# The inverse roots of all norms of a four-layer trunk: tokens across the partitions in place of tokens along the columns

## What is computed

```python
def rms_norm(x, g):
    xf = x.astype(F32)
    y = xf * lax.rsqrt(jnp.mean(xf * xf, axis=-1, keepdims=True) + EPS)
    return (y * g.astype(F32)).astype(x.dtype)
```

## Time and profile before

| | us |
|---|---|
| three timed runs | 3506.8, 3507.42, 3504.56 |
| median | 3506.8 |
| profiled execution, first to last instruction | 3502.8 |
| TensorE busy (matmul) | 3042.4 (87%) |
| TensorE busy (weight load) | 2847.5 (81%) |
| VectorE busy | 2287.8 (65%) |
| GpSimd busy | 1537.3 (44%) |
| ScalarE busy | 935.4 (27%) |

### The profile page before, as it was taken

The page is one execution under the profiler, slowest core; times in us unless marked ns, Lnnn a source line. Parts: engine busy times, 40 slices in busy tenths (PEclk is TensorE's granted clock), DMA queues, the critical chain, the costliest instruction groups (busy, mean ns, idle before and its releaser), DMA issues.

```text
span 3502.8 us, 62449 instructions
## 1 busy us (share of the span) xinstructions
PE 3042.4 (87%) x24344; PEld 2847.5 (81%) x24344; DVE 2287.8 (65%) x3035; ACT 935.4 (27%) x1276; POOL 1537.3 (44%) x670
## 2 busy tenths in 40 slices
PE   5788899999788799989454469999999999989999
PEld 5555599999788699989444469999998988789999
DVE  5566568861677758881699975888144345478850
ACT  3122233332433233332100113333221221122221
POOL 4111055565222155555445435555643332356663
PEclk9789899999899899999677779999999999999999
DMA  3001022233111122223100002222332222112232
GB/s 110 25 27 33 19 79 84 86 107 98 60 54 48 36 73 84 84 85 103 54 1 0 0 15 89 78 87 87 112 103 77 82 67 73 55 56 89 84 104 83
DMA packets 66509, 235.52 MB, mean 67 GB/s; under 512 B 8144, under 2 KB 9040, under 8 KB 65616
## 3 DMA queue, kind: packets, MB, share of 16 engines
q1 hardware_dynamic: 63648, 225.77, 21.3%
q10 hardware_dynamic: 2736, 7.94, 0.7%
HBM read 231.58 MB, written 2.10 MB: 67 GB/s over the span
## 4 chain that ended last, share of the span: by engine, by line
PE 46%; DVE 36%; issue 13%; DVEq 2%; ACT 1%; POOL 1%; DMA 0%; ACTq 0%; POOLq 0%
PE ps L224 36%; DVE scr L426 7%; DVE scr L423 6%; DVE ub L417 4%; DVE scr L420 3%; PE ps L237 2%; DVE work L1550 2%; PE ps L245 1%; PE ps L1810 1%; DVEq L420 1%; DVE work L1046 1%; PE ps L990 1%; DVE spare L1546 1%; DVE work L792 1%; DVE scr L1538 1%
## 5 line engine op out<-in xcount | busy, mean ns | idle before, releaser
L224 PE MATMUL ps<-xs,wr 128*128 128x264 f32 x13056 | 1659.5, 288 | 71.3 <-POOL xs L336 31.6
L224 PEld LDWEIGHTS ps<-xs,wr 128*128 128x128 f32 x13056 | 1623.0, 192 | 105.0 <-issue 61.5
L212 POOL TENSOR_TENSOR wr<-raw,wr 128x1024 fp32r<-128x1024 f32 x422 | 1103.5, 2617 | 1291.0 <-ACT wr L204 1288.2
L224 PE MATMUL ps<-hid,wr 128*128 128x264 f32 x6528 | 803.4, 286 | 28.2 <-POOL wr L212 13.8
L224 PEld LDWEIGHTS ps<-hid,wr 128*128 128x128 f32 x6528 | 799.0, 190 | 32.3 <-POOL wr L212 15.6
L204 ACT ACTIVATE wr<-raw 128x1024 fp32r<-128x1024 f32 x422 | 442.1, 1050 | 442.2 <-PE ps L224 438.6
L426 DVE SCALAR_TENSOR_TENSOR scr<-ub,convp,scr 128x528 f32<-128x528 f32 x176 | 469.2, 2666 | 24.0 <-DVE scr L423 0.6
L443 DVE TENSOR_TENSOR h<-ps,h 128x528 f32 x32 | 22.7, 708 | 358.1 <-PE ps L224 357.7
L487 POOL TENSOR_TENSOR hid<-scr,hid 128x528 f32 x88 | 137.3, 1561 | 222.8 <-ACT hid L459 222.8
L423 DVE SCALAR_TENSOR_TENSOR scr<-ub,convp,scr 128x528 f32<-128x528 f32 x176 | 205.2, 1166 | 26.6 <-DVE scr L420 17.4
L1363 PE MATMUL ps<-spare,work 128*128 128x256 f32 (+1 forms) x288 | 83.5, 460 | 131.5 <-ACT spare L1618 131.2
(11 more groups left out here) (265 smaller groups left out, 2643.2 us busy)
## 6 DMA issues: line engine op xcount, KB each, us to landing
raw<-in_stream SPq DMA_DIRECT2D x422, 512.0 KB, 3.6
work<-in_ret_tab ACTq DMA_DIRECT2D x4, 1056.0 KB, 5.5
h<-in_h SPq DMA_DIRECT2D x8, 264.0 KB, 5.8
out<-h SPq DMA_DIRECT2D x8, 256.0 KB, 4.6
work<-in_s_b ACTq DMA_DIRECT2D x1, 1024.0 KB, 5.1
work<-in_s_c ACTq DMA_DIRECT2D x1, 1024.0 KB, 6.8
convp<-in_convp ACTq DMA_DIRECT2D x4, 88.0 KB, 1.9
work<-in_mla_tab ACTq DMA_DIRECT2D x1, 264.0 KB, 2.6
```

The costliest lines, as they stand in the source:

```text
L212: pool.tensor_tensor(wr[:, s, 1].rearrange("p a b -> p (a b)"), raw[:, s, :], wr[:, s, 0].rearrange("p a b -> p (a b)").bitcast(F32), ALU. ...
L224: mm = pe.matmul(out[:, q], wr[:, slot, w, b0 + k], x[k][v][:, q * HALF:(q + 1) * HALF], start=start and k == 0 and p == 0, stop=stop and ...
```

## The change

`sums_pe` swaps its operands: the squares, a block of 128 tokens, are the stationary operand, and one column of ones is the moving one. The result has the tokens on the partitions, one column for each of five blocks of tokens. The last block begins at token 400, so that it overlaps the fourth. The first operand's quarters and the tile positions go. `mean_rsqrt` works on 128 x 5, or 128 x 10 for the two norms of an MLA head, and its last product is one instruction into a small tile; the memsets that cleared the old destinations go. `spread_pe` has five matmuls: the stationary operand is one column of the roots repeated 128 times by a stride of zero, the moving operand is the identity matrix, which yields each token's root on every partition in its column. The spread tile is then contiguous (528 columns), no longer two halves, and the readers' views change with it.

```diff
         def sums_pe(pe, g, col, srcs):
-            for q in range(4):
+            for b in range(COLS):
+                t0 = min(b * P, T - P)
                 for j, (src, rows) in enumerate(srcs):
-                    mm = pe.matmul(flat(g)[32 * q:32 * q + 32, col:col + QUARTER], ones[0:rows, 0:32],
-                                   src[0:rows, q * QUARTER:(q + 1) * QUARTER],
-                                   start=j == 0, stop=j == len(srcs) - 1, tile_position=(0, 32 * q))
+                    mm = pe.matmul(flat(g)[:, col + b:col + b + 1], src[0:rows, t0:t0 + P], ones[0:rows, 0:1],
+                                   start=j == 0, stop=j == len(srcs) - 1)
             return mm
 
-        def spread_pe(pe, g, quarters):
-            for q in range(2):
-                mm = pe.matmul(tile(g)[:, q], pick[:], quarters[:, q * HALF:(q + 1) * HALF], start=True, stop=True)
+        def spread_pe(pe, g, r):
+            for b in range(COLS):
+                t0, first_row = b * P, max(0, b * P - (T - P))
+                w = min(P, T - t0)
+                mm = pe.matmul(flat(g)[:, t0:t0 + w], r[:, b:b + 1].broadcast_to([P, P]), ident[:, first_row:first_row + w],
+                               start=True, stop=True)
             return mm
 
-        def mean_rsqrt(dve, g, cols, width, quarters, scratch, o, pre, r=0, free=None):
-            n = len(cols) * QUARTER
+        def mean_rsqrt(dve, g, col, n, width, dst, scratch, o, pre, r=0, free=None):
...
-            for k, c in enumerate(cols):
-                ins = dve.tensor_scalar(x[:, k * QUARTER:(k + 1) * QUARTER], flat(g)[:, c:c + QUARTER], 1.0 / width, EPS,
-                                        ALU.mult, ALU.add)
-                if k < len(cols) - 1:
-                    one(f"mean{k}", ins, False)
+            ins = dve.tensor_scalar(x, flat(g)[:, col:col + n], 1.0 / width, EPS, ALU.mult, ALU.add)
...
-            for k, dst in enumerate(quarters):
-                for q in range(4):
-                    rows, c = slice(32 * q, 32 * q + 32), slice(k * QUARTER, (k + 1) * QUARTER)
-                    one(("q", k, q), dve.scalar_tensor_tensor(dst[rows, q * QUARTER:(q + 1) * QUARTER], t[rows, c], 1.5,
-                                                              y[rows, c], ALU.add, ALU.mult), False)
+            one("r", dve.scalar_tensor_tensor(dst, t, 1.5, y, ALU.add, ALU.mult), False)
...
         def norm_dve(dve, n, g):
-            dve.memset(rstd[:], 0.0).then_inc(norm_dve_done.sem, norm_dve_done.one("clear"))
             dve.wait_ge(norm_pe_done.sem, norm_pe_done.done("sums", n))
-            dve.wait_ge(norm_dve_done.sem, norm_dve_done.done("clear", n))
-            mean_rsqrt(dve, g, [SUMS], D, [rstd], ub[:, 1, 2:], norm_dve_done, "n", n)
+            mean_rsqrt(dve, g, SUMS, COLS, D, rcol[:, 0:COLS], ub[:, 1, 2:], norm_dve_done, "n", n)
             dve.memset(sqsum[:], 0.0).then_inc(sum_cleared, 1)
             dve.wait_ge(norm_pe_done.sem, norm_pe_done.done("spread", n))
-            dve.tensor_copy(halves(rstd[:]), tile(g)).then_inc(tile_free, 1)
+            dve.tensor_copy(rstd[:], flat(g)[:, 0:T]).then_inc(tile_free, 1)
```

More of the change, by code:

```diff
@@ L39 @@
 QB = SEQ // P
-QUARTER = T // 4
 SUMS = 848
 NEWTON = ["bits", "y0", "a0", "b0", "y1", "a1", "b1", "y2", "a2", "b2"]
-RSQRT = ["mean"] + NEWTON + [("q", 0, q) for q in range(4)]
-LAST = ("q", 0, 3)
+COLS = 5
+RSQRT = ["mean"] + NEWTON + ["r"]
+LAST = "r"
 HEADS = 8
@@ L146, in trunk @@
         ident = sb("ident", [P, P])
+        rcol = sb("rcol", [P, 8])
         gains = sb("gains", [P, 2 * DEPTH, DT])
@@ L167, in trunk @@
         norm_pe_done = Order(sem("norm_pe"), ["sums", "spread"])
-        norm_dve_done = Order(sem("norm_dve"), ["clear"] + [("n", s) for s in RSQRT])
+        norm_dve_done = Order(sem("norm_dve"), [("n", s) for s in RSQRT])
         sum_cleared = sem("sum_cleared")
@@ L291, in norm_spread_pe @@
             pe.wait_ge(norm_dve_done.sem, norm_dve_done.done(("n", LAST), n))
-            spread_pe(pe, g, rstd).then_inc(norm_pe_done.sem, norm_pe_done.one("spread"))
+            spread_pe(pe, g, rcol).then_inc(norm_pe_done.sem, norm_pe_done.one("spread"))
         def first_tiles_pe(pe, n, u0, g):
@@ L514, in mla @@
             fac = work[:, 16]
-            scratch = work[:, 18:20].rearrange("p a b -> p (a b)")
-            quarters = [work2[:, (10 + k) * T:(11 + k) * T] for k in range(2)]
+            scratch = misc[:, 112:142]
+            rhead = misc[:, 100:100 + 2 * COLS]
             prob = [work[:, 26 + k] for k in range(2)]
@@ L522, in mla @@
             lsq = [work[:, 10 + k] for k in range(5)]
-            lquarters = [work[:, 15], work[:, 17]]
+            lrows = [misc[:, 144 + 8 * k:144 + 8 * k + COLS] for k in range(2)]
             groups = ((0, 3, QL), (3, 5, KVL))
-            SUM_Q, SUM_K = 512 + P, 512 + P + QUARTER
+            SUM_Q, SUM_K = 512 + P, 512 + P + COLS
             G_Q, G_QR, G_K, G_KR = 5, 6, 7, 8
@@ L542, in mla @@
             consts_in = sem("mla_consts")
-            l_dve = Order(sem("mla_l_dve"), ["clear0", "clear1"] + [(k, s) for k in range(2) for s in RSQRT] +
-                          [("norm", t) for t in (0, 1, 3)] + ["gain", "up", "down", "turned", "clearq", "cleark"])
+            l_dve = Order(sem("mla_l_dve"), [(k, s) for k in range(2) for s in RSQRT] +
+                          [("norm", t) for t in (0, 1, 3)] + ["gain", "up", "down", "turned"])
             l_act = Order(sem("mla_l_act"), [("square", t) for t in range(6)] + [("hi", t) for t in range(5)])
@@ L548, in mla @@
             p_dve = Order(sem("mla_p_dve"), ["up", "down", "turned", "vt", "vtm"] +
-                          [("f", s) for s in ["mean0"] + NEWTON + [("q", k, q) for k in range(2) for q in range(4)]] +
+                          [("f", s) for s in RSQRT[1:]] +
                           ["qr", "kn", "kr"])
@@ L602, in pe_ @@
                     pe.wait_ge(l_dve.sem, l_dve.done((k, LAST)))
-                    spread_pe(pe, g0 + 7 + k, lquarters[k]).then_inc(l_pe.sem, l_pe.one(f"spread{k}"))
+                    spread_pe(pe, g0 + 7 + k, lrows[k]).then_inc(l_pe.sem, l_pe.one(f"spread{k}"))
                 pe.wait_ge(l_pool.sem, l_pool.done(("lo", 4)))
@@ L631, in proj @@
                         k = int(s == "spreadk")
-                        pe.wait_ge(p_dve.sem, p_dve.done(("f", ("q", k, 3)), h0) + i * 2 * len(p_dve.names))
-                        spread_pe(pe, g, quarters[k]).then_inc(p_pe.sem, p_pe.one(s))
+                        pe.wait_ge(p_dve.sem, p_dve.done(("f", LAST), h0) + i * 2 * len(p_dve.names))
+                        spread_pe(pe, g, rhead[:, k * COLS:(k + 1) * COLS]).then_inc(p_pe.sem, p_pe.one(s))
                 def attend(s, j, h0, i, g):
@@ L689, in dve_ @@
                 dve.wait_ge(consts_in, 32)
-                for k in range(2):
-                    dve.memset(lquarters[k], 0.0).then_inc(l_dve.sem, l_dve.one(f"clear{k}"))
-                dve.wait_ge(l_dve.sem, l_dve.done("clear1"))
                 for k, (a0, a1, width) in enumerate(groups):
                     dve.wait_ge(l_pe.sem, l_pe.done(f"sum{k}"))
-                    mean_rsqrt(dve, g0 + 7 + k, [SUMS], width, [lquarters[k]], scratch, l_dve, k)
+                    mean_rsqrt(dve, g0 + 7 + k, SUMS, COLS, width, lrows[k], scratch, l_dve, k)
                 for k, (a0, a1, width) in enumerate(groups):
@@ L1018, in dve_ @@
                 dve.wait_ge(consts_in, 48)
-                dve.memset(quarters, 0.0).then_inc(c_dve.sem, c_dve.one("clear"))
                 L4 = [lg[:, 8 * k:8 * k + 8] for k in range(4)]
@@ L1751, in ret @@
             a_dve = Order(sem("ret_a_dve"), ["SM", "S0", "S2"] + [f"o{t}" for t in range(4)] + ["s0", "s1", "s2"] +
-                          [f"d{t}" for t in range(4)] + ["clear", "v0", "v1", "v2"] + [("f", s) for s in RSQRT] +
+                          [f"d{t}" for t in range(4)] + ["v0", "v1", "v2"] + [("f", s) for s in RSQRT] +
                           ["n0", "n1", "n2"] + [f"z{t}" for t in range(4)])
@@ L1772, in spread @@
                     pe.wait_ge(a_dve.sem, a_dve.done(("f", LAST), R))
-                    spread_pe(pe, g, fac).then_inc(a_pe.sem, a_pe.one("SPREAD"))
+                    spread_pe(pe, g, rhead).then_inc(a_pe.sem, a_pe.one("SPREAD"))
                 def attend(s, r, i, g, seq):
@@ L1906, in attend @@
                     else:
-                        mean_rsqrt(dve, g, [SUMS], RDV, [fac], ub[:, 1, 2:], a_dve, "f", R)
+                        mean_rsqrt(dve, g, SUMS, COLS, RDV, rhead, ub[:, 1, 2:], a_dve, "f", R)
                         finish(dve, R, g, i)
                 def squares(R):
-                    dve.memset(fac, 0.0).then_inc(a_dve.sem, a_dve.one("clear"))
                     for k in range(3):
```

26 lines of the change are left out of this document (12 added, 14 removed).

## The result

| | median us | range, runs |
|---|---|---|
| kernel before | 3506.5 | 3502.6 to 3513.1, 12 |
| kernel after | 3518.0 | 3511.7 to 3521.5, 12 |

The ratio is 1.0032, with a 95% interval from 1.0023 to 1.0040: the change costs 11.5 us. I had forecast 3491 us and a range that ended at 3512, so the forecast was wrong in sign. The profiled execution of after spans 3515.3 us, 12.5 more than that of before. Its mean granted clock is 0.919 where it was 0.928.

What follows compares the result with a forecast made beforehand. TensorE, busy 87% of the span, was taken as the bound, with Newton on the chain only in places. Terms summed to -16 us: span 3502.8 to 3487, plus 4 for timed runs, 3491 us; range 3472 to 3512.

Steps and rivals of the forecast that it cites:

- MLA heads, -18: MLA heads: Newton -3.7, sums +0.9 or +1.3, spreads +0.4 us; -2.4 in five heads, -2.0 in three.
- The price of the warm pair (0.32): MLA sums: one 128-row and one 64-row matmul take 0.32 us together at 2.4 GHz, 0.11 for the height change.
- The price of Newton: MLA heads: twelve small VectorE steps take 2.4 us where the chain took 6.1, -3.7 us a head.
- the clock falls in the sums: One-column sums lower the clock early: MLA +21, HGRN and retention heads +16, giving 3528 us; chance 0.18.
- the clock stays up in MLA: MLA heads: a shorter wait keeps the spreads at 2.4 GHz, a further -13 us in eight heads, 3478 us; chance 0.25.
- Cheap record: All new sums: a record costs its moving columns, 0.021 us instead of 0.107, giving 3444 us; chance 0.04.
- Small steps of 0.20 us: Newton on 5 or 10 columns: each VectorE step takes 0.20 us, twelve steps 2.4 us.
- the rival that they cost more: Retention and FFN norms: GpSimd holds small steps, returning about 5 us, 3496; with other small losses, chance 0.10.
- HGRN heads, +10 - 1.6: HGRN heads: dearer sums and spread cost 1.4 us in each of seven, +10; the last gains 1.6 from Newton.
- HGRN's, S5's and retention's block norms, -4, -0.8, -4: These three block norms: shorter Newton steps on the chain save 4, 0.8 and 4 us.
- Latent norms, -3.5: MLA's two latent norms: both Newtons end at 76.9 where they ended at 80.37, -3.5 us.
- Retention +3, four hidden norms +3: Four retention heads +0.5 to +1.2 us each; four block norms with hidden Newton pay for sums and spread; +3 each group.

Runs made afterwards that it cites:

- the ordered kernel: Kernel after with each MLA head's ten sums over 128 rows placed before its ten over 64 rows, instead of alternating: 3501.0 us, ratio 0.9988.

## Why the prediction was wrong

**MLA heads, -18: failed, and it alone turned the sign.** The step that failed is "five of the eight heads have the sums at 2.4 GHz and three at 1.2". No head ran them at 2.4 GHz throughout: one was at 1.2 from the start and the clock fell within the sums of the other seven, so that they took 69.5 us in place of 63.8. More was lost in a place where the forecast had nothing, by its words that the clock falls behind the sums "as it does now": 9.5 us behind the keys' copies, with 23.4 more us of low clock. The first loss follows the moved columns as far as the runs go: sums of one height kept 2.4 GHz in one head of eight with one column and in five with 32. The second went away in the ordered kernel already, whose sums lost the clock in seven heads; why after has it stays open. The price of the warm pair (0.32) was right: 0.112 and 0.20 us, 0.31 together. The price of Newton was right too: -29.2 for -29.6.

**What the price of the pair should have told me.** The change of height was a term of the new sums only, 0.11 us. I took before's 5.5 us in an MLA head as given, though the trace had the contradiction: 8 records in 0.36 us in a block norm, 32 in 5.47 in a head. It was there that the time lay: 43 us in the kernel before, and 17 in the kernel after.

**Rival "the clock falls in the sums", at 0.18: came true in its mechanism, by luck in its size.** It gave 3528 and decides from 3509; measured 3518. The clock did fall in the MLA sums, but late, for 5.7 us and not 21. HGRN's heads, for which it had most of a further 16, were about as forecast. Its clock that rises about 3 us later there rests on no row, and no run shows it. What filled the gap are the 9.5 us behind the heads and some 10 us in the other rows, which it doesn't name. My argument against it, that the old sums held 2.4 GHz for 5.5 us, compared unlike things: those move 132 columns a record, the new one moves one.

**Rival "the clock stays up in MLA": false.** It built on a wait of TensorE of 1.4 us before the spread. That wait is filled by T, O, T at the low clock, and all pairs of spreads in the MLA heads of after take 4.3 to 4.5 us.

**Cheap record: false.** 0.112 us for the 128-wide load with one moving column, in every block norm that runs at 2.4 GHz. By the table in the Trainium skill (TensorE: Matmul & The Clock Gate, Back-to-back issue gap) it would be 0.025. But the same section says that its gap is that of a single matmul and that "at small N it under-counts (no LDWEIGHTS budget, ~56 ns vs 81 measured)". These sums are such a case, with a new 128-column stationary for each record, and I should have seen that the table doesn't price them.

**Small steps of 0.20 us: the price was right,** twelve in 2.4; the rival that they cost more is false in the rows above.

**HGRN heads, +10 - 1.6; HGRN's, S5's and retention's block norms, -4, -0.8, -4: right** within 1 us between the marks (+9.9 with the next norm's part, -3.5, -0.8, -4.7). For S5's a part is luck: in two kernels with the new root there and the old one in HGRN's heads its row was +3.7 and +3.9, in two more of that kind -0.6. In the last HGRN head, from its sums to the use of its spread, 0.4 us came rather than 1.6 (7.5 to 7.2): its sums ran at 1.2 GHz, 2.29 us for 0.43.

**Latent norms, -3.5:** 0.7 us at their first use and 1.7 at the first head's sums, counted from the norm's copy, because their stream too went over to 1.2 GHz behind record 22. With 64 columns it was 3.4 at the first use.

**Retention +3, four hidden norms +3: too small in this trace**, +6.1, +2.0 at the start, +1.6 and +4.0. Retention's row can't be put down to the root: with the old one in its heads it was +4.0 and +3.7 in two kernels and -2.0 to -2.2 in three. In FFN 3, every fourth projection tile comes another 0.4 us later until the total is 4.0; every kernel with the new root in that norm has it (4.0 or 4.1, six kernels), every one with the old has -0.2 to 0. It starts with a VectorE operation that takes 2.69 us beside GpSimd's work at another point (the second tap, L412, instead of the third, L426 before), but what keeps it up I haven't shown. Why the low clock comes back in stretches of 10.2 us behind the heads is open too.

## What to carry to other kernels

Before replacing a slow piece ask why it is slow: here one comparison of two call sites of the same helper (8 records in 0.36 us, 32 in 5.47) was worth 43 us, where the change cost 11.5. A matmul which moves one column cost its weight load here, 0.112 us a record, and a long stream of such matmuls lost the clock; more columns that fitted beside the load cost nothing in the latents and kept it. The gain of a part is not the gain of the stage: look at the clock of what follows, and at a second kernel with the same code there, before you believe a difference of a few us. Where an engine "waits" in the chain, look at what it does in that wait before you price a shorter one.

## What the runs showed of the hardware

- Loads between matmuls of different height (128 and 64 rows) wait for the matmul in front: 0.20 us from load to load with one moving column, 0.23 with 32, 0.25 with 64, against 0.112 with the height unchanged, all at 2.4 GHz and with 128-column stationaries. With 32-column stationaries and 132 moving columns it is 0.31, and the change also keeps the column groups from working together: 5.47 us for 32 records, 1.24 without it.
- Of two streams with the same 50 loads 0.112 us apart, both starting at 1.00, the one with one moving column went to 0.50 behind record 22, the one with 64 columns kept 1.00. Over all kernels the first kind lost the clock in five of five, the second in none of six. In MLA heads with ordered sums 32 columns kept it in five of eight (in two kernels), one column in one of eight.
